# Sixteen cache copies over four blocks of a feed-forward stage: two, two, six, six in place of four each

## What is computed

```
q, k, v, u = split(modulated_rms_norm(x) @ w_in)
att   = merged dilated window attention(q, k, v)       # samples: over cache + 4 new rows
ssm   = S5 state space(u), GELU, GLU
x1    = x + gate1 * (concat(norm(att), norm(ssm)) @ w_out)
h2    = modulated_rms_norm(x1)
y     = x1 + gate2 * ((silu(h2 @ w_gate) * (h2 @ w_up)) @ w_down)
k_sample = concat(cache_k, k)[:, 4:]      # and v_sample from cache_v
```

## Time and profile before

| | |
|---|---|
| median of 3 runs | 2680.95 us (2677.60 to 2681.61) |
| profiled execution | 2676.8 us, of which the span is 2675.0 us |
| TensorE busy | 2568.2 us, 96% of the span |
| DVE, ScalarE, GpSimd busy | 74%, 48%, 19% |
| mean granted TensorE clock | 0.983 of full |
| blocks 0 and 1 | about 1290 to 1761 us |
| round 0 of the down projection | about 1762 to 1982 us |
| blocks 2 and 3 | about 1982 to 2448 us |
| round 1 | about 2449 us to the end |
| the 16 copies | at the starts of pairs 1, 4, 6 and 9 of each block; 14.3 to 15.8 us from issue to landing |

### The profile page before, as it was taken

One profiled execution on the slowest core, in us unless ns is written; L12 is line 12 of the kernel. 1 busy time (PEld: TensorE's weight loads), 2 busy tenths in 40 slices (PEclk: granted clock), 3 DMA queues, 4 the chain that ended last, 5 costly groups with the idle time before them and its releaser, 6 DMA issues.

```text
span 2675.0 us, 46742 instructions
## 1 busy us (share of the span) xinstructions
PE 2568.2 (96%) x17757; PEld 2210.4 (83%) x17757; DVE 1982.7 (74%) x3672; ACT 1284.8 (48%) x2509; POOL 499.4 (19%) x621
## 2 busy tenths in 40 slices
PE   5999999999999999999799999989999999999998
PEld 3678887777787778878799999978889999998787
DVE  6647887557767548677899999956588899886546
ACT  4212221338789646656454545534445555554343
POOL 2106787440001000000113222110000000000000
PEclk8999999999999989999899999999999999999999
DMA  9663333853433896444799779897568867888664
GB/s 338 200 203 113 122 122 134 292 173 123 129 120 111 321 362 215 145 147 135 239 320 283 246 246 290 266 313 238 192 213 268 249 213 220 266 262 288 232 216 159
DMA packets 407081, 583.52 MB, mean 218 GB/s; under 512 B 35105, under 2 KB 295969, under 8 KB 396866
## 3 DMA queue, kind: packets, MB, share of 16 engines
q1 hardware_dynamic: 383144, 440.50, 51.0%
q0 software_dynamic: 21264, 139.16, 15.6%
q10 hardware_dynamic: 2450, 0.87, 0.1%
HBM read 447.76 MB, written 199.27 MB: 242 GB/s over the span
## 4 chain that ended last, share of the span: by engine, by line
PE 64%; DVE 7%; ACT 3%; issue 2%; DMA 1%; SPq 1%; DVEq 0%; ACTq 0%
PE f_ps L2869 27%; PE f_ps L2911 15%; PE c_ps_w L2165 7%; PE a_o_ps L406 2%; PE a_s_ps L377 2%; PE a_t_ps L388 2%; DVE f_ws L3055 2%; PE c_ps_glu L2140 2%; PE b_ps_t L1787 1%; ACT a_probs L444 1%; PE a_o_ps L414 1%; PE b_ps_s L1799 1%; PE b_ps_o L1824 1%; DVE f_s L3063 1%; PE a_t_ps L357 1%
## 5 line engine op out<-in xcount | busy, mean ns | idle before, releaser
L2869 PE MATMUL f_ps<-f_x,f_ws 128*128 128x256 f32 (+1 forms) x7392 | 906.6, 285 | 33.4 <-DVE f_sl L3118 20.1
L2869 PEld LDWEIGHTS f_ps<-f_x,f_ws 128*128 128x128 f32 x7392 | 901.2, 191 | 45.0 <-issue 38.9
L2911 PE MATMUL f_ps<-f_ws 128*128 128x512 f32 x1848 | 423.9, 391 | 12.6 <-DVE f_ws L3055 9.2
L2911 PEld LDWEIGHTS f_ps<-f_ws 128*128 128x128 f32 x1848 | 348.7, 189 | 88.4 <-DVE f_ws L3055 9.6
L946 PE MATMUL p_out_ps<-p_w,p_hT 128*128 128x512 f32 x1620 | 379.8, 392 | 1.1 <-DVE p_qk L1222 1.1
L3055 DVE TENSOR_TENSOR f_ws<-f_raw,f_ws 128x1024 fp32r<-128x1024 f32 x208 | 268.1, 1295 | 132.6 <-ACT f_ws L2972 132.4
L946 PEld LDWEIGHTS p_out_ps<-p_w,p_hT 128*128 128x128 f32 x1620 | 300.9, 188 | 73.1 <-issue 11.6
L3055 DVE TENSOR_TENSOR f_ws<-raw,f_ws 128x1024 fp32r<-128x1024 f32 x210 | 262.7, 1257 | 117.7 <-ACT f_ws L2972 117.4
L2972 ACT ACTIVATE f_ws<-raw 128x1024 fp32r<-128x1024 f32 x210 | 220.9, 1057 | 210.7 <-PE f_ps L2911 106.8
L2972 ACT ACTIVATE f_ws<-f_raw 128x1024 fp32r<-128x1024 f32 x208 | 218.8, 1057 | 215.0 <-PE f_ps L2911 106.6
L444 ACT ACTIVATE a_probs<-a_probs,a_o 128x256 f32<-128x256 f32 (+1 forms) x384 | 171.1, 451 | 1.4 <-DVE a_o L487 1.4
(11 more groups left out here) (381 smaller groups left out, 3800.5 us busy)
## 6 DMA issues: line engine op xcount, KB each, us to landing
scratch_aF<-f_stage SPq DMA_DIRECT2D x44, 896.0 KB, 6.6
out_dram<-in_cache_k_dram POOLq DMA_DIRECT2D x8, 4088.0 KB, 14.7
out_dram<-in_cache_v_dram POOLq DMA_DIRECT2D x8, 4088.0 KB, 14.5
raw<-in_w_gate_dram SPq DMA_DIRECT2D x88, 256.0 KB, 5.3
raw<-in_w_up_dram SPq DMA_DIRECT2D x88, 256.0 KB, 5.5
f_raw<-in_w_gate_dram SPq DMA_DIRECT2D x88, 256.0 KB, 5.3
f_raw<-in_w_up_dram SPq DMA_DIRECT2D x88, 256.0 KB, 5.7
raw<-scratch_aF SPq DMA_DIRECT2D x78, 256.0 KB, 3.3
```

The source lines that it names most:

```text
L2869: mm = pe.matmul(ps[bank][:, 0:w], ws[s % SLOTS][:, y, j * 512 + k * 128:j * 512 + (k + 1) * 128], x_half(b, p, z)[:, k], start=(p < 3 and ...
L2911: mm = pe.matmul(ps[bank][:, :], slot[:, y, j * 128:(j + 1) * 128], slot[:, z, 512:1024], start=(p < 3 and k == 0 and x == 0), stop=(k == ...
```

## The change

The copies are the same sixteen in the same order. Blocks 0 and 1 now issue two each, in pairs 3 and 8; blocks 2 and 3 issue six each, in pairs 1, 3, 5, 6, 8 and 10. Pairs 5 and 6 are neighbours.

```diff
         all_stored(pool, h2_stored)
         all_stored(pool, x1_stored)
+        moved = 0
         for b in range(FB):
             r = b // 2
             for n in range(NPAIRS):
                 g = b * NPAIRS + n
                 if g:
                     pool.wait_ge(product, 4 * g)
-                if n in (1, 4, 6, 9):
-                    move(4 * b + (1, 4, 6, 9).index(n))
+                if n in ((3, 8) if b < 2 else (1, 3, 5, 6, 8, 10)):
+                    move(moved)
+                    moved += 1
                 if r == 0:
                     t_step(g)
                 if b % 2 == 0 and 6 <= n < 10:
```

## The result

The changed kernel is slower. Five runs gave a median of 2696.57 us (2688.9 to 2701.6) against 2680.95 for the kernel before; the ratio is 1.0059, with a 95% interval of 1.0037 to 1.0082, so 10 to 22 us. Three more rounds on another occasion gave 1.0051 (1.0029 to 1.0074). The profiled execution took 2688.9 us, 12.1 more than that of before (2676.8), and was the fastest of its five.

The account below looks back on a forecast made before the run. TensorE was taken to set the length, with DMA hidden but nearly full in block 3. 2676.8 - 1.6 + 9.5 + 0.5 + 2.3 = 2687.5 us profiled, 2691 against the median; range for 8 in 10: 2677 to 2699.

Parts of the forecast that it names:

- First half: Blocks 0 and 1, copies taken away: TensorE gaps sum to -1.55, about -1.6 us, range +1 to -5.
- the very effect I credited at g = 5: Block 0, g = 5: subtractions waited for a load queued behind the copy of g = 4; 0.81 us gained.
- a twin without a copy: g = 7, gap 3.76 us, no copy in its pair; so nothing taken for the 3.70 gap at g = 9.
- Collision in block 3: Pairs 5 and 6: store lands behind second copy, DVE waits 10 us, TensorE loses 9.5 us, bounds 0 and 14.5; 0.57.
- my limit of 13.66 us: DVE, last product to fifth product's additions: up to 13.66 us costs TensorE nothing, each further us costs one.
- Block 2: Pairs 5 and 6: DVE waits 1 to 2 us for the store, forgiven; 0.5 us, bounds 0 and 7.
- my reason for block 2: Block 2, pairs 5 and 6: store goes out 2 us ahead of the second copy, not 0.5 behind.
- Last copy: Block 3, pair 10: copy delays SyncE's load for the tenth down piece by 3.5 us; 2.3 us, bounds 0 and 5.
- My estimate from that rule: DMA queues while a copy runs: SyncE left 15% of the bytes, 0.7 MB per copy.
- that no collision happens: Rival, block 3: store keeps pace with the copy, DVE waits no more than forgiven 2.0 us; about 2681 us, chance 0.27.
- The rival that block 2 collides as well: Block 2, where the store goes out 2 us ahead, collides too: 7 us more, about 2698 us, chance 0.07.

## Why the prediction was right, step by step

I forecast 2691 us and slower at 0.60; the median was 2696.57, the profiled execution 2688.9 against a sum of 2687.5. The direction, the place and the way of the main loss were as forecast. That the sum comes within 1.4 us is in part luck: its terms are off by -1.0, +2.1, -0.5, -0.6 and +1.2 us, and the second profiled execution of the same kernel took 2702.52.

- **First half, forecast -1.6, measured -2.6, of which 0.4 was there before the first gap** (its first long run starts at 1307.33, before at 1307.72). By gaps: g = 5 gone, g = 17 gone, g = 3 at 1.24 (forecast 1.17), g = 19 new at 1.18 (forecast 1.17): right. g = 15 was forecast gone and is 1.06: the subtractions there waited for the load behind the copy of g = 14. That is the very effect I credited at g = 5 and forgot to charge where the copy went. Not counted either: g = 1 gone (before 1.10), g = 7 from 3.76 to 3.00 and g = 9 from 3.70 to 2.66, and against them a new 1.20 in block 1, pair 9, where DVE waited 3.29 us for the store behind the copy of g = 19. I had called g = 7 a twin without a copy, but a copy stood in the pair before it, at g = 6, and is worth 0.8 us there. The gap at g = 9 is 2.65 to 3.83 us in executions with the same positions, so its gain is not the change's. The errors nearly cancel.
- **Collision in block 3, forecast 9.5, measured 11.6.** Each step held: the store behind the copy, DVE's wait in pair 6, the break ahead of the seventh product. Two terms were off. The store landed at 2365.5, the DVE wait was 13.0 us and not 10: it had not gone out 0.5 us behind the copy but 1.27, and what was ahead of it in SyncE's queue was caught too. And TensorE forgave 13.03 - 9.76 = 3.3 us and not 2.0: my limit of 13.66 us was read in block 1, while in block 3 it is 2369.44 - 2344.76 - 9.76 = 14.92. Of the 1.26 us between them, 1.06 can be the sample products, which TensorE does there ahead of the seventh product; no run takes them away. The clock afterwards cost 1.8, forecast 1.5.
- **Block 2, forecast 0.5 with bounds 0 and 7.** Nothing in the first profiled execution, about 11.9 us in the second, beyond my bound: a gap of 7.34 us at pair 3, one of 1.62 at pairs 5 and 6, and slower matmuls behind. At pair 3 the copy follows the seven activation loads that SyncE sends out around 2027 to 2038. I looked for neighbouring copies and left out that other load on the same queue, although the deadline was the same. And my reason for block 2, a store 2 us ahead of the copy, does not protect it: one 3.05 us ahead took 14.9 us. This is the term that I sized too small, and it makes the changed kernel's executions uneven.
- **Last copy, forecast 2.3, measured 1.7**: gaps of 2.48 and 2.31 us in place of 3.40. The step held: SyncE's load for the tenth piece went out 2468.98 - 2458.94 = 10.0 us into round 1 in place of 2454.74 - 2448.57 = 6.2, so 3.9 us later, forecast 3.5. But the size is no constant: round 1 took 226.3 to 226.5 us in the six profiled executions without this copy and 225.5 to 229.7 in the seven with it.
- **Not forecast: round 0, +1.2 us**, its gap 9.59 in place of 9.21 us and the run behind it 182.16 for 181.38. I had nothing for it, and no run tells why. Five profiled executions with this first half took 220.74 to 221.72 us in round 0 and three with that of before 220.53 to 220.66, so the sign holds and the size does not.

The Trainium skill's rule (DMA: Bandwidth & Descriptors, section on queues, rings and completion order) is that each DMA engine takes turns between queues packet by packet. The trace agrees: 70 packets of SyncE's beside 48 of the copy's. My estimate from that rule, 15% of the bytes or 0.7 MB per copy, was too high by about ten times; the rows show about 1%. I had divided by the mean packet of GpSimd's queue, 6.5 KB, and this mixes the copies with its many smaller packets. The trace of the kernel before had the right number, from 2306 to 2318 us with one copy:

```profile
q0 software_dynamic: 64, 4.19, 107.0%
```

That is 65 KB per packet. The sum did not use the estimate.

Of the rivals, that no collision happens is excluded in block 3: all four profiled executions with these positions unedited there (two of the changed kernel, the one with neighbours in block 3 alone, the one with block 2 cleared) lose time in pairs 6 and 7. The rival that block 2 collides as well, at 0.07, came true in one of the two profiled executions of the changed kernel, so its chance was set too low. The profiled execution was 12.1 us slower and the medians 13.8 and 15.6; the difference of 2 to 3 us lies inside the intervals, and whether block 2 fills it stays open.

## What to carry to other kernels

A background copy that is free on average has a place: ask at each position what the other queue issues in the next microseconds and what it still has under way, and by when the engines need it. Distance between copies counted here, not their number; one neighbouring pair in block 3 cost 12 us where one copy more per block cost none. When you ask what share a queue gets, read the packets of the transfer itself, in the stretch in which it runs, and not the mean of its queue. And put the issue of a background transfer behind the load and the work of the same engine that others wait for: with the positions to suit, that gave 5 us against the kernel before; the runs don't separate the two.

## What the runs showed of the hardware

- While a 4088 KB copy of GpSimd's queue ran, SyncE's queue moved 70 packets and 0.04 MB in 8 us beside the copy's 48 packets and 3.14 MB, with three transfers waiting.
- A 896 KB store of SyncE's queue landed in 7.1 us when issued 1.92 us ahead of such a copy and in 18.9 us when issued 1.55 us ahead. I had taken what is issued first as served first.
- The lead does not order the times: 2.49 us ahead took 6.9 us, 3.05 took 14.9, 3.4 took 12.4, 4.8 took 8.4 and 7.2 took 6.6. In the changed kernel's block 3 a 256 KB load at 2343.97 landed in 5.3 us and the next, at 2345.00 and so 0.47 us ahead of the copy, in 15.5 us.
- After a gap of 9.76 us TensorE's granted clock was at 0.88 in that stretch of 25 us, and 120 matmuls took 1.8 us more. After a gap of 2.97 to 3.04 us at g = 7, 336 matmuls took 40.05 or 40.06 us in three executions and 41.37 to 41.85 in six.
